# A fused mixer layer: which input projections are summed first, and who computes the gate rows

## The reference

```
shift, scale, gate = split(silu(c) @ w_ada + b_ada)
h    = x * (1 + scale) + shift
proj = h @ w_in + b_in          # q,k,v,z of attention | q,k,v,o,z,i,f of an mLSTM | two merge gates
A    = (stick_breaking(q, k, v) * silu(z)) @ w_sb_proj             # 8 heads of 64, in pairs
B    = (norm(mLSTM(silu(conv(q, k)), v, i, log_sigmoid(f))) * sigmoid(o) * silu(z)) @ w_ml_proj
x    = LayerNorm(alpha * x + (1 + gate) * ((sigmoid(gA) * A + sigmoid(gB) * B) @ w_out))
```

## Time and profile before

| | us |
|---|---|
| median of 3 runs | 951.34 |
| profiled execution, whole | 953.3 |
| its span | 951.6 |
| PE busy in the span | 924.0 |
| DVE busy | 610.9 |
| ACT busy | 440.6 |
| POOL busy | 167.7 |

### The profile page before, as it was taken

One profiled execution on the slowest core, in us unless ns is written; L12 is line 12 of the kernel. 1 busy time (PEld: TensorE's weight loads), 2 busy tenths in 40 slices (PEclk: granted clock), 3 DMA queues, 4 the chain that ended last, 5 costly groups with the idle time before them and its releaser, 6 DMA issues.

```text
span 951.6 us, 12863 instructions
## 1 busy us (share of the span) xinstructions
PE 924.0 (97%) x4958; PEld 756.9 (80%) x4958; DVE 610.9 (64%) x1057; ACT 440.6 (46%) x719; POOL 167.7 (18%) x118
## 2 busy tenths in 40 slices
PE   4899999999999999999999999999999999999996
PEld 3667888888888888888888888888888888878885
DVE  5838886756976748966659867534653333345997
ACT  2544766543676544665446665525742222243100
POOL 1020132230322310232311322302100000002210
PEclk9899999999999999999999999999999999999998
DMA  9921211112211113111122111127712121215232
GB/s 272 335 44 34 67 34 34 34 46 67 67 30 38 25 55 100 24 45 34 34 68 66 45 34 35 34 56 246 228 46 56 45 55 46 89 44 188 89 133 88
DMA packets 90392, 73.95 MB, mean 78 GB/s; under 512 B 4664, under 2 KB 81592, under 8 KB 90332
## 3 DMA queue, kind: packets, MB, share of 16 engines
q1 hardware_dynamic: 85380, 58.32, 22.4%
q0 software_dynamic: 2496, 8.47, 2.7%
q10 hardware_dynamic: 2456, 6.34, 1.8%
HBM read 64.59 MB, written 8.40 MB: 77 GB/s over the span
## 4 chain that ended last, share of the span: by engine, by line
PE 92%; DMA 3%; DVE 3%; SPq 1%; ACT 1%; issue 1%; DVEq 0%; ACTq 0%
PE bank L668 49%; PE bank L646 9%; PE bank L647 9%; PE bank L648 9%; PE bank L817 4%; PE bank L805 3%; DMA a_raw<-in_w_ada 2%; PE bank L792 2%; PE bank L775 2%; PE bank L794 1%; PE bank L793 1%; PE bank L829 1%; PE bank L836 1%; PE bank L840 1%; PE bank L843 1%
## 5 line engine op out<-in xcount | busy, mean ns | idle before, releaser
L668 PE MATMUL bank<-hH,wH 128*128 128x512 f32 x688 | 271.3, 394 | 3.0 <-DVE wL L1443 1.7
L668 PE MATMUL bank<-hL,wH 128*128 128x512 f32 x688 | 271.1, 394 | 0.0
L668 PE MATMUL bank<-hH,wL 128*128 128x512 f32 x688 | 271.0, 394 | 0.0
L606 POOL TENSOR_TENSOR ez<-ez,rem 128x512 f32<-128x512 f32 x72 | 134.6, 1882 | 392.5 <-DVE rem L1629 392.5
L1443 DVE SCALAR_TENSOR_TENSOR wL<-w_raw,wH 128x512 fp32r<-128x512 f32 x116 | 99.2, 859 | 109.6 <-ACT wH L1001 108.4
L668 PEld LDWEIGHTS bank<-hH,wH 128*128 128x128 f32 x688 | 129.2, 188 | 32.9 <-issue 3.7
L668 PEld LDWEIGHTS bank<-hH,wL 128*128 128x128 f32 x688 | 129.3, 188 | 28.8 <-issue 2.9
L668 PEld LDWEIGHTS bank<-hL,wH 128*128 128x128 f32 x688 | 129.3, 188 | 28.5 <-issue 2.9
L1001 ACT ACTIVATE wH<-w_raw 128x512 fp32r<-128x512 f32 x116 | 72.5, 627 | 103.7 <-PE bank L648 70.6
L1629 DVE TENSOR_TENSOR_SCAN rem<-rem,ones 128x512 f32<-128x512 f32 (+2 forms) x96 | 99.9, 1092 | 31.7 <-ACT rem L1108 31.7
L1096 ACT ACTIVATE ez<-bank 128x512 f32<-128x512 f32 x72 | 39.1, 596 | 99.8 <-PE bank L794 99.8
(11 more groups left out here) (260 smaller groups left out, 1483.6 us busy)
## 6 DMA issues: line engine op xcount, KB each, us to landing
w_raw<-in_w_in SPq DMA_DIRECT2D x104, 256.0 KB, 2.9
a_raw<-in_w_ada SPq DMA_DIRECT2D x12, 512.0 KB, 7.2
raw<-in_w_ada POOLq DMA_DIRECT2D x8, 512.0 KB, 5.3
x_in<-in_x SPq DMA_DIRECT2D x8, 512.0 KB, 4.1
out_y<-res SPq DMA_DIRECT2D x7, 512.0 KB, 2.9
x_rows<-in_x SPq DMA_DIRECT2D x3, 1024.0 KB, 10.4
raw<-in_w_out SPq DMA_DIRECT2D x10, 256.0 KB, 4.4
next_vg<-in_w_ada SPq DMA_DIRECT2D x4, 512.0 KB, 7.7
```

The costliest lines, as they stand in the source:

```text
L606: g.tensor_tensor(e, e, r, ALU.mult).then_inc(a_done[h], 1)
L668: ins = t.matmul(banks(number)[half][:], w, a, start=(r == 0), stop=(r == JOB_MM // 2 - 1))
```

## The change

PE no longer adds q and k to the running sums over the first four tiles, but v and z (`early`). Their sums over tiles 0 to 3 are then copied from PSUM to SBUF by ACT, four copies of 128x512 (`part`, in a buffer of w_ada that is free by then). After that PE sums q and k over tiles 0 to 3 at once (`lower`, 48 matmuls), and over tiles 4 to 7 as these come (`tile_of`). Last come v and z over tiles 4 to 7 (`late`, 24 matmuls each). DVE adds part, PSUM and bias (`whole_sum`). The order of the weight chunks and loads follows the list `PRO`.

The gate rows are shared out. POOL computes i-b into two groups of rows, ACT negates m within its exponential, and ACT, no longer DVE, makes kH and qH of the first pair. The transposes of `r_q` move behind the first scores, and DVE's copies of them (`token_columns`) behind the convolution of the second half. The exponential of z comes after `head_columns` (`first_gate`).

```
-PRO_K = 3
+PRO = [("if", 0), ("v", 0), ("z", 0), ("if", 1), ("q", 0), ("k", 0), ("q", 1), ("k", 1), ("v", 1), ("z", 1)]
@@ POOL
+            pool.wait_ge(b_scanned, 1)
+            for r in (slice(0, 32), slice(96, 128)):
+                g.tensor_tensor(r_q[r, :], r_i[r, :], r_b[r, :], ALU.subtract).then_inc(tok_done, 1)
             pool.wait_ge(bm_made, 1)
@@ PE
-            for d in range(0, KT, 2):
-                tile_of(d, 1)
...
-            for n in range(PRO_K, PRO_JOBS):
-                project(0, 0, JOB_MM, base_job=n, other_banks=1 if n == PRO_K else 0)
-            gate_columns()
+            early(0, "v")
+            ada_columns(1)
+            early(0, "z")
...
+            early(3, "vz")
+            turn_x(5)
+            lower("q", 0)
+            lower("q", 1)
+            lower("k", 0)
+            gate_rows(4)
+            ada_columns(4)
+            turn_x(6)
+            lower("k", 1)
+            turn_x(7)
+            for name in "qk":
+                tile_of(4, name)
+            gate_rows(6)
...
+            late("v")
+            late("z")
@@ PE, iteration
                     scores(i, s)
+                    if i == 0 and s == 0:
+                        gate_columns()
                     project(i, start, middle)
@@ ACT, after tile 3
+                    act.wait_ge(ada_summed, BLOCK_OF[d + 1] + 1)
+                    for n, name in enumerate("vz"):
+                        for half in range(2):
+                            act.wait_ge(part_filled, 2 * n + half + 1)
+                            a.activation(part_of(name, half), pro_banks[name][half][:], ACT.Copy)\
+                                .then_inc(part_drained, 1)
@@ ACT, after tile 7
+            pair_copy("q", next_q)
+            act.wait_ge(rows_in, 16 * 4)
+            a.activation(r_e[:], r_f[:], ACT.Exp, scale=-1.0).then_inc(f_ln, 1)
+            act.wait_ge(f_ln, 1)
+            a.activation(r_e[:], r_e[:], ACT.Ln, bias=1.0).then_inc(f_ln, 1)
+            pair_copy("k", next_k)
+            pro_split(10)
...
+            a.activation(kH[:], next_k[:], ACT.Copy).then_inc(pair_split, 1)
+            a.activation(qH[:], next_q[:], ACT.Copy).then_inc(pair_split, 1)
+            pro_split(11)
@@ DVE
+            def whole_sum(name, dst):
...
+                    v.scalar_tensor_tensor(out=dst[:, halves(half)], in0=pro_banks[name][half][:],
+                                           scalar=cols[:, 4 * (n - 1):4 * (n - 1) + 1], in1=part_of(name, half),
+                                           op0=ALU.add, op1=ALU.add).then_inc(drained[half], 1)
             row_logs()
-            pro_split(PRO_CHUNKS + 3)
+            pro_split(10)
+            dve.wait_ge(part_drained, 4)
+            whole_sum("v", next_v)
+            pro_split(11)
             row_columns()
...
+            whole_sum("z", next_g)
@@ DVE, iteration
                     if s == 0:
                         conv_sum(i, 1)
+                        if i == 0:
+                            token_columns()
+                            head_tokens(i)
```

More of the change, by code:

```diff
@@ L315, in build_kernel @@
         r_i, r_f, r_e = rt("r_i", [P, S]), rt("r_f", [P, S]), rt("r_e", [P, S])
-        r_b, r_m, r_q = rt("r_b", [P, S]), rt("r_m", [P, S]), rt("r_q", [P, S])
+        r_b, r_q, r_m = rt("r_b", [P, S]), rt("r_q", [P, S]), rt("r_m", [P, S])
         r_one = rt("r_one", [P, S])
@@ L451, in halves, with part_of @@
             return slice(h * HALF, (h + 1) * HALF)
+        def part_of(name, half):
+            return part[:, ("v", "z").index(name) * S + half * HALF:("v", "z").index(name) * S + (half + 1) * HALF]
         GROUP = {"sbq": 0, "sbk": 1, "sbv": 2, "sbz": 3, "mlq": 4, "mlk": 5, "mlv": 6, "mlo": 7, "mlz": 8}
@@ L661, in project @@
                     if r == 0:
-                        pe.wait_ge(drained[half], number - other_banks)
+                        pe.wait_ge(drained[half], number - (1 if number == PRO_JOBS else other_banks))
                     if r == 0 and number == J_GATES + 1:
@@ new lines, in _, with pair_copy @@
+            act.wait_ge(bias_in, 16)
+            act.wait_ge(rows_zero, 5)
+            bias_copy(r_if[0:2 * NH, halves(0)], 0, 0, r_bias[0:2 * NH, :], pro_ps[0][0])
+            act.wait_ge(if_moved, 2)
+            bias_copy(r_if[0:2 * NH, halves(1)], 1, 0, r_bias[0:2 * NH, :], r_if[0:2 * NH, halves(1)])
+            def pair_copy(name, dst):
+                n = PRO_NAMES.index(name)
+                for half in range(2):
+                    bias_copy(dst[:, halves(half)], half, n, cols[:, 4 * (n - 1):4 * (n - 1) + 1],
+                              pro_banks[name][half][:])
@@ new lines, in _ @@
+            pair_copy("q", next_q)
[5 more added lines that the diff above has]
+            pro_split(10)
+            for half in range(2):
+                act.wait_ge(drained[half], PRO_NAMES.index("k") + 1)
+            a.activation(kH[:], next_k[:], ACT.Copy).then_inc(pair_split, 1)
@@ new lines, in _, with first_gate @@
+            a.activation(qH[:], next_q[:], ACT.Copy).then_inc(pair_split, 1)
+            pro_split(11)
+            for q, (src, scale) in enumerate([(r_m, -1.0), (r_q, 1.0), (r_q, 1.0)]):
+                r = [slice(64, 96), slice(32, 64), slice(96, 128)][q]
+                act.wait_ge(q_rows, q + 1)
+                a.activation(r_q[r, :], src[r, :], ACT.Exp, scale=scale).then_inc(q_exp, 1)
+            def first_gate():
+                for half in range(2):
+                    act.wait_ge(drained[half], PRO_JOBS)
+                    a.activation(sig[:, halves(half)], next_g[:, halves(half)], ACT.Exp, scale=-1.0)\
+                        .then_inc(sig_exp, 1)
@@ L1488, in _ @@
             low_h(3)
-            for g in range(3, PRO_CHUNKS):
+            for g in range(3, 6):
                 pro_split(g)
@@ L1495, in _ @@
             low_h(5)
+            for g in (6, 7):
+                pro_split(g)
             mod_columns(4)
@@ L1498, in _ @@
             low_h(7)
-            for g in range(PRO_CHUNKS, PRO_CHUNKS + 3):
+            for g in (8, 9):
                 pro_split(g)
@@ L1555, in _, with token_columns, head_tokens @@
             dve.sem_inc(yml_stored, credit)
-            dve.sem_inc(bm_made, 1)
             link.base, link.k = link.base + link.k, 0
+            def token_columns():
+                for b in range(2):
+                    dve.wait_ge(m_filled[b], M_PRO[b])
+                    src = misc_ps[b][:].rearrange("p (c q r) -> p c q r", c=4, q=4)[:, :, :, 0:NH]
+                    v.tensor_copy(tok[:, 4 * b:4 * b + 4], src).then_inc(m_drained[b], 1)
+                dve.wait_ge(dec_filled, 1)
+                v.tensor_copy(dec[:].rearrange("p c h -> p h c"),
+                              misc_ps[2][:, 0:NH * NC].rearrange("p (h c) -> p h c", h=NH))\
+                    .then_inc(dec_drained, 1)
+                dve.wait_ge(dec_drained, 1)
+                for b in range(2):
+                    dve.wait_ge(m_drained[b], M_PRO[b])
+            def head_tokens(i):
+                link.mark(v.tensor_copy(h_tok[:], tok[:, :, :, bass.ds(i, 1)].rearrange("p c q a -> p q (c a)")))
+                link(v.tensor_copy(h_dec[:], dec[:, :, bass.ds(i, 1)].rearrange("p c a -> p (c a)")))
             def head_columns(i, last):
```

245 lines of the change are left out of this document (122 added, 123 removed).

## The result

The changed kernel took 953.35 us (median of 9 runs, 952.51 to 956.39), the kernel before 951.34 (9 runs, 951.0 to 953.31). The ratio is 1.0021, with a 95% interval of [1.0012, 1.0029]: slower by some 2 us, and the interval lies on both sides of the 0.2% that count as no change. The forecast was 951.8, within 0.2%, with a range up to 954.0. The measured time lies inside this range, but above the forecast's own 951.0 to 952.7.

What follows compares the result with a forecast made beforehand. PE was taken as the bound, never waiting from v's transposes in iteration 0 on, whose start DVE's list sets. Transposes 0.3 us earlier and a clock fall of 0.8 gave +0.5 on 951.34: 951.8, range 947.8 to 954.0.

Steps and rivals of the forecast that it cites:

- the price of POOL: Behind the r_b scan, POOL's two subtractions hold DVE's wL: 2.1 us, then 0.8, together 2.9; bounds nothing to 4.3.
- T: Start of v's transposes in iteration 0, from which PE never waits; forecast at 106.1 instead of 106.43, 0.3 us earlier.
- The slower rival: POOL's second subtraction costs its full 2.1 because v's sums are held too, and the clock falls in full: 954.0; chance 0.17.
- The faster one: POOL on 32 partitions holds DVE not at all or shortly; DVE ready 2.9 us earlier, time 948.9; chance 0.31.
- The wait before iteration 0: PE's gap ahead of iteration 0, which it starts at 83.9 once v's first half is summed: 2.5 us.
- ACT's part copies: Prologue: four copies at 0.6 us push h of tiles 4 and 5 back some 3 us, hidden by 36 matmuls.
- DVE's stretch: DVE's list from the row logs at 73.9 up to v's transposes: 32.2 us, before 34.4.
- The wait at T: PE reaches v's transposes at 102.3 and waits there 3.8 us for DVE.
- The term of 0.8: PE's clock falls behind the 3.8 us gap at v's transposes, costing 0 to 1.6 us; half taken.
- The prediction's own signs of being wrong: wL beside POOL takes 0.7 us, PE doesn't wait for tok, or another wait over 1 us appears behind 110 us.
- the anchor: Differences of the profiled span, 951.6, are put on the timed median, 951.34, the two being near by chance.
- PE's 6.4 us: Ahead of v's transposes, PE could give back three gaps of 4.8 us and 1.6 us of slow clock.

Runs made afterwards that it cites:

- pool_zeros: Changed kernel without POOL's two subtractions i-b, their rows set to zero ahead, so part of the gates is left out; 950.28 us, ratio 0.9989 to the kernel before.
- pool_half_rows: Changed kernel with POOL's two subtractions over 512 of 1024 columns, the other half zero; 951.63 us, ratio 0.9996 to the kernel before.
- copies_spread: Changed kernel with ACT's two copies of z's parts moved behind h of tile 4; 951.42 us, ratio 1.0002 to the kernel before.
- tok_early: Changed kernel with DVE's copies of tok and dec ahead of the second half's convolution; 952.25 us, ratio 1.0001 to the kernel before.
- rows_undone: Changed kernel with the gate rows made by DVE alone again and POOL subtracting nothing; 955.89 us (5 runs), ratio 1.0038 to the kernel before.
- i_minus_b_on_dve: Changed kernel with POOL's subtractions replaced by one on DVE and a 32-row copy on ACT; 952.42 us, ratio 1.0008 to the kernel before.
- before_again: The kernel before, unedited, timed and profiled once more; 951.53 us, ratio 1.0002, profiled span 949.8.

## Why the prediction held, and where it did not

**Right: what decides, and the price of POOL.** In the changed kernel T is set by DVE's list between the gate rows and tok. Where that list was made shorter (pool_zeros, pool_half_rows) or began earlier (copies_spread), T came earlier by as much. The two subtractions cost 2.9 us (2.12 + 0.74 measured; with them left out the list is 2.86 shorter). The sums of v between them took 1.41 for two, as the sums of z did when POOL was idle (1.40 at 93.24). So they are not held. For this the prediction had only the Trainium skill, SBUF — State Buffer, "Who interferes with whom": a VectorE instruction with at most one SBUF input passes. The sums have one operand in PSUM and one long one in SBUF, and the trace agrees. The slower rival, which rested on a hold of these sums, falls, although its 954.0 lies nearer to the measured time than the forecast: its mechanism isn't there. The faster one falls too, since 32 partitions hold DVE just as 128 do. The wait before iteration 0 (2.65, forecast 2.5) and DVE's two waits (1.20 and 0.40, forecast 1.2 and 0.5) came as well.

**Wrong by 1.4: ACT's part copies were costed at nothing.** The step took the 36 matmuls of `lower` as their cover. But `turn_x(5)` stands ahead of these on PE's list, and it waits for ACT's h of tile 4, which the copies hold up until 42.23. That was PE's gap of 1.45. The gate rows ended at 63.16 and not 61.8, f landed at 73.05 and not 71.7, the row logs began at 75.24 and not 73.9. copies_spread gives the 1.4 back.

**Wrong by 1.0 the other way: DVE's stretch.** It was forecast at 32.2 and is 31.2 (75.24 to T). One `wL` fewer stands in it: five, where the window of rows 5 holds six. That is 0.7 of it. The remaining 0.3 is spread over small rows. That the two errors almost cancel is luck: T was forecast at 106.1 and measured at 106.43. (Two small slips don't matter here: 42.9 + 8.3 is 51.2 and not 51.3, and POOL's second subtraction at its full 2.1 in place of 0.8 adds 1.3 and not 1.4.)

**Wrong in the placing: PE's wait and the clock.** The wait at T was put at 3.8 and is 0.85. PE started iteration 0 at 85.33, 1.4 later than forecast. It lost some 1.8 in the slow stretch behind its gap of 2.65: it reached the transposes at 105.58, 20.25 later, where the forecast has 18.4 (83.9 to 102.3) and tok_early, whose clock stays at 1.00 there, takes 18.49. The clock is 0.72 from 84 to 90 us. The forecast had the slow stretch behind T, where it costs time. In the changed kernel it stands ahead of T and costs nothing, because PE has to wait there anyway. The term of 0.8 is thus 0 here. rows_undone and i_minus_b_on_dve show the forecast's case: a wait of 2.8 to 3.1 at T, and 1.2 to 1.6 us for it, where the term allowed 0 to 1.6. The prediction's own signs of being wrong cover this only in part: PE did wait for tok, but for 0.85 and not 3 to 4, and the gap that should have gone came back as 1.45 at tile 5's transposes.

**Wrong by 2: the anchor.** This is the step that made 951.8 out of what should have been 953. The prediction says that the span of 951.6 is "by chance near the median of the three timed runs", and puts its difference of 0.5 on 951.34. But the 951.6 is a span, and that execution took 953.3, 2.0 above the median; its T lies 1.8 later than that of before_again, mostly by the slow stretch at 45 us. Forecast T was 106.1. With 845.1 behind it and 1.7 around the span that makes 952.9, and the measured median is 953.35. The prediction even counted the slow stretch's 1.6 among what PE could get back, without asking whether the timed runs had it. The chance of slower, 0.17, was too low for the same reason.

**Where PE's 6.4 us went.** In before_again, whose time is that of a usual execution, 1.6 of them had never been lost, for the clock doesn't fall at 45 us. Of the gaps (4.7 in before_again, 1.79 + 1.29 + 1.61) PE got back all, and lost 1.45 to ACT's copies, 2.65 at iteration 0, 1.8 to the slow clock behind that, and 0.85 at T. That is 6.75, and the 4.7 with the 1.8 by which T moved (104.61 to 106.43) make 6.5. The last 0.25 isn't traced.

## What to carry to other kernels

Before putting a difference on a median, compare the profiled execution's whole time with the timed runs: the 2 us too many there were mostly a second slow stretch of the clock, and they were as large as the whole effect. The same holds for an experiment's trace: that of tok_early is of its fastest run, that of rows_undone of one of its two faster ones. A reordering that frees one engine is worth only as much as the engine behind it can follow. Here PE's 4.7 us ended as waits for DVE, whose list between one landing and one copy set the end. A cover has to be read in the order of the waiting engine: copies are not hidden by matmuls that stand behind the next instruction that needs the copying engine. If a wait can't be removed, its place matters, since a slow stretch of PE behind an early wait runs while PE would wait anyway.
